# The first gate product in two halves: contraction over four feature blocks at a time, with the context's transposes between its heads

## The chip, the cores and the metric
One core of a Trainium2 chip runs the whole program in one launch. The time is the device time of an execution in microseconds; lower is better. TensorE (PE) multiplies, VectorE (DVE), ScalarE (ACT) and GpSimd (POOL) do the rest, and SyncE (SP) and GpSimd issue the DMAs. All data are float32.

## The reference
Two transformer blocks with adaptive modulation follow each other. Only the head of the first one matters here. 256 latent tokens `x` and 256 context tokens `ctx`, each 1024 wide, are normalised and modulated by a shift and a scale that come from a conditioning vector, and then multiplied by the columns of `w_in`:

```python
mod_lat = jax.nn.silu(c) @ w_ada[l] + b_ada[l]
mod_ctx = jax.nn.silu(c_ctx) @ w_ada[l] + b_ada[l]
sh1, sc1, gt1, sh2, sc2, gt2 = jnp.split(mod_lat[:, None, :], 6, axis=-1)
...
h_lat = modulate(rmsnorm(x_lat, norm_pre_mix[l]), sh1, sc1)      # h * (1 + scale) + shift
h_ctx = modulate(rmsnorm(x_ctx, norm_pre_mix[l]), csh1, csc1)
...
da_q, da_k, da_v, hg_ff, hg_fb, hg_i, hg_q, hg_g = jnp.split(h_lat @ w_in, SPLITS, axis=-1)
...
f = lb + (1.0 - lb) * jax.nn.sigmoid(z.astype(jnp.float32))      # the forget gate of hg_ff and hg_fb
```

After it come a gated recurrence and a differential attention in parallel, an output product, 16 experts with expert-choice routing, and then a second network (latent attention and a Fourier mixer) on the result.

## The kernel before
**Tiles.** Weights come in tiles of 1024 rows by 512 columns (2 MB), as eight blocks of 128 rows, into a ring of slots; the early part uses slots 0 to 3 in turn. `("ada", i)` is the i-th 512 columns of the modulation weights: ada 0 and 1 are the shift of features 0 to 511 and 512 to 1023, ada 2 and 3 the scale of the same halves. `("in", t)` is a tile of `w_in`; in 3 and in 4 are the gates of the two directions of the recurrence. SyncE walks `stream` in order (L664). For a tile that reuses a slot it first waits until the last reader of the tile before has filled its bank. Before: ada 0, 1, 2, 3, in 3, ada 6, in 4, ada 7, in 6, ada 8, in 5 and on.

**Conditioning.** `mod_product(i)` (L813) multiplies the silu of the conditioning by tile ada i on TensorE: 16 matmuls. ScalarE copies the result (`take_mod`, L1380); `mod_columns(i)` on TensorE (L824) turns it into columns, and on VectorE (L1722) adds the bias. `fold` (L1729) makes the scale ready, once for the latent set `MIX`, once for the context set `MIXC`.

**The activations.** x is normalised, turned by TensorE (`turn_input`, `turn_chunks`, L803: 16 transposes of 128x128) and copied to `hT`, feature blocks j = 0 to 7 on the partitions. When the modulation is known, VectorE modulates hT in place, eight operations of 128x256 (L1739), and signals `hT_ready`.

**The order on TensorE** (the program below in short):

```python
turn_input(0)
for i in FIRST_MODS:            # 0, 1, 2, 3
    mod_product(i)
    if i:
        mod_columns(i - 1)
...
for d in range(2):              # w_in tiles 3 and 4
    heads_out(("z", d, hp), w, (2 * hp, 2 * hp + 1), lat, T)
    if d == 0:
        turn_input(1)           # the context's transposes
    tokens_out(("zc", d, b), w, hT3, TB + b)
    mod_step(d)                 # products of ada 6, then ada 7
```

`heads_out` makes the gate of two heads in one bank, 2 x 8 matmuls of 128x256 (L794), contraction over all eight blocks of hT. `tokens_out` makes the context's gate zc, token block by token block, with 128x512 matmuls. The context's transposes are copied out of their banks, already modulated, by ScalarE (L1363, blocks 0 to 3) and VectorE (L1701, blocks 4 to 7).

**Behind it.** ScalarE takes the exponential of z and zc; VectorE makes sigmoids (a reciprocal of 128x1024 takes 6.55 us), the running sums and 1 - f; ScalarE takes logarithms (L1407, L1409). From those TensorE makes the triangle sums `dsum`, the first matmuls with `pair` as operand (L794 at 125.03). GpSimd computes the reciprocal roots of the norms and, once the last of the first ada tiles has landed, loads ctx, the rows of the lower bound, the lambda rows, subln, hgn and the mask.

**Banks.** PSUM has eight banks; `claim(name, b)` fixes at build time the order in which results take a bank, `pclaim` goes round banks 0 to 3. An engine that takes a bank waits until its last content was read.

Of the kernel before, what the change touches and what calls it, by code (L numbers as in the profile page):

```python
# [12 lines left out]
P = 128  # L13
# [97 lines left out]
FIRST_MODS = [0, 1, 2, 3]  # L111
# [22 lines left out]
def block_program(nc, a, out):  # L134
    ctx = ExitStack()
    with ctx:
# [91 lines left out]
        def mod_tile(i):  # L228
            l, o = divmod((i - 12) * TN, 3 * D)
            tile(("ada", i), wtile(a["w_ada"][0], i * TN) if i < 12 else wtile(a["w_ada_2"][l], o))  # L230

        for i in FIRST_MODS:
            mod_tile(i)

        order = iter(COLUMN_MODS)
        for t in (3, None, 4, None, 6, None, 5, None, None, 1, None, None, 0, None, None, None, None, 7, 2, None):
            if t is None:
                mod_tile(next(order))
            else:
                tile(("in", t), wtile(w_in, t * TN))  # L240
# [27 lines left out]
        def place(name, s):  # L268
            slot_of[name], turn_of[name] = s, slot_uses[s]
            slot_uses[s] += 1  # L270

        occupants = {}
        turn = 0
        for name, _ in stream:
            if name[0] == "kvctx":
# [90 lines left out]
        for i in FIRST_MODS:  # L366
            claim(("mod", i), i)
            claim(("modT", i), 4 + i)
# [6 lines left out]
        def claim_gate(d):  # L375
            for hp in range(2):
                pclaim(("z", d, hp))
            if d == 0:
# [14 lines left out]
        claim_mod(0)  # L393
# [305 lines left out]
        def _(pool):  # L699
# [26 lines left out]
            pool.wait_ge(landed[FIRST_MODS[-1]], 16)  # L726
# [64 lines left out]
        def _(pe):  # L791
# [56 lines left out]
            def turn_input(s):  # L848
                for b in range(TB):
                    pe.wait_ge(sem("normed"), 2 * s + b + 1)  # L850
                    for g in range(2):
                        turn_chunks(("xT", s, b, g), (tm3, cx3)[s][:, b, :], g)

            turn_input(0)
            pe.wait_ge(sem("silu_c"), 1)
            for i in FIRST_MODS:
                mod_product(i)
                if i:
                    mod_columns(i - 1)
            mod_columns(FIRST_MODS[-1])  # L860

            pe.wait_ge(sem("hT_ready"), 1)
# [13 lines left out]
            for d in range(2):  # L876
                w = wait_tile(pe, ("in", 3 + d))
                for hp in range(2):
                    heads_out(("z", d, hp), w, (2 * hp, 2 * hp + 1), lat, T)
                if d == 0:  # L880
                    turn_input(1)
                    for b in range(TB):
                        for g in range(2):
                            wait_copied(pe, ("xT", 1, b, g))
                for b in range(TB):
                    tokens_out(("zc", d, b), w, hT3, TB + b)
                mod_step(d)
# [451 lines left out]
        def _(act):  # L1339
# [56 lines left out]
            for d in range(2):  # L1396
                for hp in range(2):
                    o = wait_filled(act, ("z", d, hp))
                    frees(st, act.activation(kg[d][:, hp * TN:(hp + 1) * TN], o[:, :], ACT.Exp, scale=-1.0),
                          ("z", d, hp))  # L1400
# [4 lines left out]
                take_mod(COLUMN_MODS[d])  # L1405
# [253 lines left out]
        def _(dve):  # L1659
# [66 lines left out]
            def fold(s, norm, signal):  # L1726

                st.settle()
                step(dve.scalar_tensor_tensor(mc[:, s, 1, :], mc[:, s, 1, :], 1.0, norm, ALU.add, ALU.mult), signal)  # L1729
                st.settle()  # L1730

            for i in FIRST_MODS:
                mod_columns(i)
            fold(MIX, colof("pre_mix"), None)
            fold(MIXC, colof("pre_mix"), "mc_ready")
            wait_copied(dve, ("xT", 0, 1, 0))
            st.settle()
            for j in range(J):
                step(dve.tensor_scalar(hT3[:, j, 0:T], hT3[:, j, 0:T], mc[:, MIX, 1, j:j + 1], mc[:, MIX, 0, j:j + 1],  # L1739
                                       ALU.mult, ALU.add), "hT_ready" if j == J - 1 else None)  # L1740
# [47 lines left out]
            for d in range(2):  # L1788
                wait_copied(dve, ("z", d, 0))
                wait_copied(dve, ("z", d, 1))  # L1790
# [509 lines left out]
```

## Time and profile before
| | us |
|---|---|
| median of three runs | 1204.85 (1204.59 to 1205.53) |
| the profiled execution | 1199.85 |
| its span in the trace | 1198.0 |
| TensorE busy | 943.8 (79%) |
| VectorE busy | 300.7 (25%) |
| ScalarE busy | 210.6 (18%) |
| GpSimd busy | 45.5 (4%) |
| mean granted TensorE clock | 0.918 of full speed |
| moved by DMA | 310.46 MB, 259 GB/s over the span |

The profiled execution is a run of its own, 5 us shorter than the median. Its span leaves out 1.85 us at the ends. Everything between 480 and 890 us is the experts' loop, which waits for their weights; the change is in the first 80 us.

### The profile page before, as it was taken

The numbers are of one execution on the slowest core, as the hardware profiler recorded it, in microseconds if no ns is written. First come the engines' busy times: TensorE is split into PE (matmuls) and PEld (weight loads), VectorE is DVE, ScalarE is ACT, GpSimd is POOL, SyncE is SP. The second block draws the span as 40 slices with busy tenths as digits, with TensorE's granted clock in tenths as the row PEclk, the third lists the DMA queues.
The fourth block names the chain that finished last, engine by engine and source line by source line (L and its number), as shares of the span: only waits on it lengthen the run. The fifth ranks groups of instructions, "written<-read, shape, count | busy, mean of one in ns | idle before, by whom it ended". The sixth has DMA issues, their size and how long they took to land.

```text
span 1198.0 us, 11068 instructions
## 1 busy us (share of the span) xinstructions
PE 943.8 (79%) x4392; PEld 491.1 (41%) x4392; DVE 300.7 (25%) x551; ACT 210.6 (18%) x429; POOL 45.5 (4%) x98
## 2 busy tenths in 40 slices
PE   4799989999898769665666666566566988989987
PEld 2666454754544355121212212122124845534843
DVE  1299233570451333000000000000003134330002
ACT  2223221321352212000000000000003134210010
POOL 0200000000100100000000000000001000000000
PEclk9899989999899869888888888888888999999999
DMA  9943441771988309999999999999995441041000
GB/s 353 348 155 141 176 145 67 270 292 71 329 297 350 140 9 413 418 429 428 429 429 429 429 428 428 428 428 429 428 414 208 178 159 43 1 141 71 1 1 35
DMA packets 65367, 310.46 MB, mean 259 GB/s; under 512 B 2705, under 2 KB 4932, under 8 KB 52916
## 3 DMA queue, kind: packets, MB, share of 16 engines
q1 hardware_dynamic: 62836, 301.04, 62.8%
q0 software_dynamic: 2496, 8.93, 2.1%
q8 instruction: 24, 0.39, 0.1%
q14 instruction: 11, 0.09, 0.0%
HBM read 308.91 MB, written 1.05 MB: 259 GB/s over the span
## 4 chain that ended last, share of the span: by engine, by line
PE 59%; DMA 28%; DVE 6%; issue 2%; ACT 2%; SPq 1%; POOL 1%; POOLq 0%; ACTq 0%; DVEq 0%
PE bank L794 41%; DMA ring<-w_up_dram 27%; PE bank L1127 8%; PE bank L813 3%; DMA ring<-w_ada_dram 2%; PE bank L925 1%; PE bank L824 1%; PE bank L803 1%; SPq L664 1%; PE bank L1145 1%; PE bank L1259 1%; PE bank L977 1%; PE bank L1282 1%; PE bank L1158 1%; PE bank L832 1%
## 5 line engine op out<-in xcount | busy, mean ns | idle before, releaser
L1127 PE MATMUL bank<-ring,ilat 128*32 128x512 f32 x960 | 147.1, 768 | 107.4 <-DMA ring<-w_up_dram 107.3
L1127 PEld LDWEIGHTS bank<-ring,ilat 128*32 128x32 f32 x960 | 40.9, 135 | 211.8 <-issue 211.8
L794 PE MATMUL bank<-ring,kT 128*128 128x512 f32 (+1 forms) x224 | 97.7, 597 | 5.4 <-DVE kT L1701 3.4
L794 PE MATMUL bank<-ring,hT 128*128 128x512 f32 x224 | 98.8, 601 | 1.7 <-DVE hT L1701 1.7
L2131 DVE TENSOR_TENSOR state<-state,bank 64x512 f32<-64x512 f32 x16 | 11.0, 690 | 329.3 <-ACT state L1571 329.3
L794 PE MATMUL bank<-hT,ring 128*128 128x256 f32 (+1 forms) x320 | 86.5, 431 | 3.6 <-DVE hT L1739 3.6
L794 PEld LDWEIGHTS bank<-hT,ring 128*128 128x128 f32 x320 | 61.8, 195 | 28.3 <-issue 17.7
L1145 PE MATMUL bank<-ring,ilat 128*32 128x512 f32 x512 | 62.8, 633 | 11.8 <-ACT ilat L1575 11.8
L1571 ACT ACTIVATE state<-bank 64x512 f32<-64x512 f32 x16 | 9.5, 592 | 332.6 <-PE bank L1127 332.6
L794 PEld LDWEIGHTS bank<-ring,kT 128*128 128x128 f32 x224 | 43.1, 194 | 58.2 <-issue 58.2
L794 PEld LDWEIGHTS bank<-ring,hT 128*128 128x128 f32 x224 | 43.0, 193 | 55.6 <-issue 53.6
L1158 PE MATMUL bank<-state,ilat 128*128 128x512 f32 x120 | 55.1, 601 | 13.6 <-DVE state L2135 13.6
L794 PE MATMUL bank<-kT,ring 128*128 128x256 f32 x256 | 55.7, 379 | 0.0
L813 PE MATMUL bank<-ring,act 128*32 128x512 f32 x384 | 49.4, 636 | 6.7 <-DMA ring<-w_ada_dram 3.0
L794 PEld LDWEIGHTS bank<-kT,ring 128*128 128x128 f32 x256 | 48.6, 190 | 7.3 <-issue 0.8
L1158 PEld LDWEIGHTS bank<-state,ilat 128*128 128x128 f32 x120 | 21.6, 189 | 48.3 <-issue 48.3
L803 PE MATMUL bank<-const,pair 128*128 128x128 f32 x112 | 20.1, 339 | 26.6 <-DVE pair L2068 18.9
L1145 PEld LDWEIGHTS bank<-ring,ilat 128*32 128x32 f32 x512 | 15.8, 115 | 47.2 <-issue 41.9
L2135 DVE COPY state<-bank 128x512 f32<-128x512 f32 x16 | 11.1, 692 | 89.8 <-PE bank L1145 89.8
L803 PEld LDWEIGHTS bank<-const,pair 128*128 128x128 f32 x112 | 16.9, 181 | 30.7 <-DVE pair L2068 20.2
L1136 PE MATMUL bank<-const,state 128*128 128x128 f32 x64 | 11.8, 308 | 21.5 <-DVE state L2131 21.5
L794 PE MATMUL bank<-ring,gates 128*128 128x512 f32 x64 | 27.7, 593 | 1.1 <-DVE gates L2249 1.1
(315 smaller groups left out, 1007.9 us busy)
## 6 DMA issues: line engine op xcount, KB each, us to landing
ring<-w_down_dram SPq DMA_DIRECT2D x32, 2048.0 KB, 24.0
ring<-w_gate_dram SPq DMA_DIRECT2D x32, 2048.0 KB, 18.8
ring<-w_up_dram SPq DMA_DIRECT2D x32, 2048.0 KB, 23.3
ring<-w_ada_dram SPq DMA_DIRECT2D x24, 2048.0 KB, 11.4
ring<-w_in_dram SPq DMA_DIRECT2D x8, 2048.0 KB, 12.1
ring<-fno_w_in_dram SPq DMA_DIRECT2D x4, 2048.0 KB, 8.1
ring<-w_out_dram SPq DMA_DIRECT2D x2, 2048.0 KB, 8.3
ring<-mla_w_in_dram SPq DMA_DIRECT2D x2, 2048.0 KB, 21.8
```

What stands on the lines that cost most here:

```text
L664: sp.dma_start(slot_view(s, src.shape[1], src.shape[2]), src).then_inc(landed[s], 16)
L794: ins = pe.matmul(o, l, r, start=start and i == 0, stop=stop and i == len(terms) - 1)
L803: ins = pe.transpose(o[:, jj * P:(jj + 1) * P], chunk, ident)
L813: ins = pe.matmul(o[32 * q:32 * q + 32, :], act_cols[i // 12][:, j, :], w[:, j, :], start=jj == 0, stop=jj == 1)
L824: ins = pe.matmul(o[:, 2 * jj:2 * jj + 2], chunk, C("sum_columns"), start=True, stop=True)
L832: fills(pe.matmul(o[:, :], C("sum_columns")[:, 0:1].broadcast_to([P, P]), modr_of(i), start=True, stop=True), ("gt", i))
L925: ins = pe.matmul(o[:, k * P:(k + 1) * P], keys[:, c:c + P], queries[:, c:c + P], start=True, stop=True)
L977: fills(pe.matmul(o[i][:, :], q3[ps, h, b * P:(b + 1) * P], k3[ps, h, :], start=True, stop=True), ("s", b, h, i))
L1127: ins = pe.matmul(bank[0][32 * t:32 * t + 32, :], x[:, j, :], w[2 * half + t // 2][:, j % JH, n0:n0 + TN], start=j == 0, stop=j == J - 1)
L1145: ins = pe.matmul(bank[2 + n][32 * q:32 * q + 32, :], hmT[:, q, 32 * c:32 * c + 32], w[4 + c][:, q, n * TN:(n + 1) * TN], start=c == 0, st ...
L1158: ins = pe.matmul(bank[4 + 2 * b + n][:, :], m[:, b * P:(b + 1) * P], yb[n], start=first, stop=last)
L1259: fills(pe.matmul(o[:, :], ckv_all[:, b * P:(b + 1) * P], wvh[:, 4 * g:4 * g + 4, P:2 * P], start=True, stop=True), ("v2", b, g))
```

## The change
The first four ada tiles come in the order 0, 2, 1, 3, and in 3 is loaded in the third place. Shift and scale of features 0 to 511 are then known first: VectorE folds and modulates blocks 0 to 3 of hT, and TensorE contracts these four blocks for all four heads of the gate z(0), into four banks (0, 1, 5, 6) that stay open. With ada 1 and ada 3 the same is done for blocks 4 to 7, which completes the sums. After head 1 and after head 3 of this second half TensorE turns one token block of the context each. The product of ada 6 goes ahead of zc(0). in 3 stays in its slot beyond ada 6, so the slots of the later tiles are worked out by what is used up first. GpSimd's loads wait for ada 1 instead of ada 3 by name; both have the fourth place in the queue.

```diff
-FIRST_MODS = [0, 1, 2, 3]
+FIRST_MODS = [0, 2, 1, 3]
...
-        for i in FIRST_MODS:
-            mod_tile(i)
+        mod_tile(FIRST_MODS[0])
+        mod_tile(FIRST_MODS[1])
+        tile(("in", 3), wtile(w_in, 3 * TN))
+        mod_tile(FIRST_MODS[2])
+        mod_tile(FIRST_MODS[3])
...
-        for t in (3, None, 4, None, 6, None, 5, None, None, 1, None, None, 0, None, None, None, None, 7, 2, None):
+        for t in (None, 4, None, 6, None, 5, None, None, 1, None, None, 0, None, None, None, None, 7, 2, None):
...
-        turn = 0
+        tiles = [name for name, _ in stream if name[0] != "kvctx"]
+        used_up = [name for name in tiles if name != ("in", 3)]
+        used_up.insert(used_up.index(("ada", COLUMN_MODS[0])) + 1, ("in", 3))
...
-                place(name, turn % EARLY_SLOTS)
-                turn += 1
+                place(name, k if k < EARLY_SLOTS else slot_of[used_up[k - EARLY_SLOTS]])
...
-            claim(("mod", i), i)
-            claim(("modT", i), 4 + i)
+            claim(("mod", i), 2 + k % 2)
+            claim(("modT", i), (4, 7)[k % 2])
...
+                for h in range(HEADS):
+                    claim(("z", d, h), (0, 1, 5, 6)[h])
+                pb[0] = 2
...
+                claim(("mod", COLUMN_MODS[0]), 4)
...
-            pool.wait_ge(landed[FIRST_MODS[-1]], 16)
+            ada1 = ("ada", FIRST_MODS[2])
+            pool.wait_ge(landed[slot_of[ada1]], 16 * (turn_of[ada1] + 1))
...
+            def first_gate(h, half):
+
+                o = pe_take(pe, ("z", 0, h)) if half == 0 else bank[turns[("z", 0, h)][0]]
+                ins = sum_of(o[:, 0:T], [(w3[:, j, h * P:(h + 1) * P], lat[j])
+                                         for j in range(4 * half, 4 * half + 4)],
+                             start=half == 0, stop=half == 1)
+                if half:
+                    fills(ins, ("z", 0, h))
+
+            for half in range(2):
+                pair_of = FIRST_MODS[2 * half:2 * half + 2]
+                for i in pair_of:
+                    mod_product(i)
+                for i in pair_of:
+                    mod_columns(i)
+                w3 = wait_tile(pe, ("in", 3))
+                pe.wait_ge(sem("hT_ready"), half + 1)
+                for h in range(HEADS):
+                    first_gate(h, half)
+                    if half and h % 2:
+                        turn_input(1, h // 2)
+            mod_step(0)
+            for b in range(TB):
+                for g in range(2):
+                    wait_copied(pe, ("xT", 1, b, g))
+            for b in range(TB):
+                tokens_out(("zc", 0, b), w3, hT3, TB + b)
...
+                n = TN if d else T
+                for i in range(1024 // n):
+                    o = wait_filled(act, ("z", d, i))
+                    frees(st, act.activation(kg[d][:, i * n:(i + 1) * n], o[:, 0:n], ACT.Exp, scale=-1.0),
+                          ("z", d, i))
+                if d == 0:
+                    take_mod(COLUMN_MODS[0])
...
+            for half in range(2):
+                js = slice(4 * half, 4 * half + 4)
+                for i in FIRST_MODS[2 * half:2 * half + 2]:
+                    mod_columns(i)
+                fold(MIX, colof("pre_mix"), None, js)
+                if half == 0:
+                    wait_copied(dve, ("xT", 0, 1, 0))
+                for j in range(4 * half, 4 * half + 4):
+                    step(dve.tensor_scalar(hT3[:, j, 0:T], hT3[:, j, 0:T], mc[:, MIX, 1, j:j + 1],
+                                           mc[:, MIX, 0, j:j + 1], ALU.mult, ALU.add),
+                         "hT_ready" if j == 4 * half + 3 else None)
+                fold(MIXC, colof("pre_mix"), "mc_ready" if half else None, js)
```

## Rows read from the trace of the kernel before
**Rows 1.** The page: span, and the chain that ended last, by engine.
```profile
span 1198.0 us, 11068 instructions
...
PE 59%; DMA 28%; DVE 6%; issue 2%; ACT 2%; SPq 1%; POOL 1%; POOLq 0%; ACTq 0%; DVEq 0%
```
**Rows 2.** TensorE's waits from 0 to 140 us: total, times, longest.
```profile
PE bank L794 <- DVE hT L1739: 3.6, 1, 3.6
PE bank L813 <- DMA ring<-w_ada_dram: 3.0, 2, 2.2
```
**Rows 3.** The chain in order of time, 10 to 76 us: start, us, what.
```profile
10.16 20.07 DMA ring<-w_ada_dram
...
37.69 16.21 PE bank L794 x64
...
58.83 15.67 PE bank L794 x32
```
**Rows 4.** The timeline, 18 to 91 us: start, us, what [idle before <- releaser].
```profile
17.98 3.69 PE L813 MATMUL bank<-ring,act 128*32 128x512 f32 x32
...
24.86 3.60 PE L813 MATMUL bank<-ring,act 128*32 128x512 f32 x16 [2.21 <-DMA ring<-w_ada_dram]
...
30.28 1.92 PE L813 MATMUL bank<-ring,act 128*32 128x512 f32 x16 [0.83 <-DMA ring<-w_ada_dram]
...
33.05 1.03 PE L824 MATMUL bank<-const,modr 128*128 128x2 f32 x8
...
34.96 2.67 DVE L1739 TENSOR_SCALAR hT<-hT,modc 128x256 f32<-128x256 f32 x8
...
37.69 4.55 PE L794 MATMUL bank<-hT,ring 128*128 128x256 f32 x10 [3.61 <-DVE hT L1739]
...
43.57 1.42 DVE L1693 TENSOR_SCALAR pair<-pair,small 128x1024 f32<-128x1024 f32 x2 [5.94 <-POOL small L720]
...
53.73 1.04 PE L803 MATMUL bank<-const,pair 128*128 128x128 f32 x8
...
76.28 14.08 PE L794 MATMUL bank<-hT,ring 128*128 128x256 f32 x64
...
90.20 13.90 PE L794 MATMUL bank<-ring,hT 128*128 128x512 f32 x32
```
**Rows 5.** SyncE's issues of in 3, ada 6, in 4: start, and time to landing.
```profile
L664 SPq DMA_DIRECT2D ring<-w_in_dram x1: 373/373/373, 20.0 to 20.0; - x1
DMA to landing us min/median/max: 16.6/16.6/16.6
...
L664 SPq DMA_DIRECT2D ring<-w_ada_dram x1: 5036/5036/5036, 21.7 to 21.7; - x1
DMA to landing us min/median/max: 31.8/31.8/31.8
...
L664 SPq DMA_DIRECT2D ring<-w_in_dram x1: 4283/4283/4283, 28.5 to 28.5; - x1
DMA to landing us min/median/max: 30.5/30.5/30.5
```
**Rows 6.** Two stretches: busy time by engine, granted clock, DMA share, GB/s.
```profile
41.00:42.00 1.00, 1.00 (x4) 0.82 (x3) 0.00 (x0) 0.97 (x3) 0.00 (x0) 0.50 1.04 403
42.00:43.00 1.00, 1.00 (x6) 0.85 (x6) 0.00 (x0) 0.32 (x2) 0.42 (x2) 0.99 1.01 379
```
**Rows 7.** VectorE's chain: hgn's landing, its ends in the timeline, its wait.
```profile
L735 POOL DMA_DIRECT2D hgn<-hg_norm_dram x1: 537/537/537, 35.0 to 35.0; - x1
DMA to landing us min/median/max: 15.5/15.5/15.5
...
57.21 1.36 DVE L1701 TENSOR_SCALAR hT<-bank,modc 128x128 f32<-128x128 f32 x4 [1.03 <-PE bank L803]
...
115.77 1.06 ACT L1409 ACTIVATE pair<-pair 128x1024 f32<-128x1024 f32 x1 [5.08 <-DVE pair L1805]
...
125.03 0.30 PEld L794 LDWEIGHTS bank<-pair,const 128*128 128x128 f32 x2 [0.84 <-issue]
...
DVE ring L1820 <- ACT ring L1417: 6.5, 2, 5.2
```

More of the change, by code:

```diff
@@ L365, in block_program @@
                 claim(("xT", 0, b, g), 2 + g)
[L366 to L368 removed]
+        for k, i in enumerate(FIRST_MODS):
+            claim(("mod", i), 2 + k % 2)
+            claim(("modT", i), (4, 7)[k % 2])
         pb = [0]
@@ L375, in claim_gate @@
         def claim_gate(d):
-            for hp in range(2):
-                pclaim(("z", d, hp))
-            if d == 0:
+            if d:
+                for hp in range(2):
+                    pclaim(("z", d, hp))
+            else:
+                for h in range(HEADS):
+                    claim(("z", d, h), (0, 1, 5, 6)[h])
+                pb[0] = 2
                 for b in range(TB):
@@ L847, in _, with turn_input @@
             fills(pe.transpose(o[:, 0:N_BIAS], bias_rows, ident[0:N_BIAS, 0:N_BIAS]), "bias_rows")
[L848 to L854, printed above, removed]
-            pe.wait_ge(sem("silu_c"), 1)
[L856 to L862, printed above, removed]
+            def turn_input(s, b):
+                pe.wait_ge(sem("normed"), 2 * s + b + 1)
+                for g in range(2):
+                    turn_chunks(("xT", s, b, g), (tm3, cx3)[s][:, b, :], g)
+            for b in range(TB):
+                turn_input(0, b)
+            pe.wait_ge(sem("silu_c"), 1)
             def heads_out(name, w, hs, rhs, n):
@@ L875, in _ @@
             lat = [hT3[:, j, 0:T] for j in range(J)]
[L876 to L887, printed above, removed]
+            def first_gate(h, half):
[19 more added lines that the diff above has]
+            for b in range(TB):
+                for g in range(2):
+                    wait_copied(pe, ("xT", 1, b, g))
+            for b in range(TB):
+                tokens_out(("zc", 0, b), w3, hT3, TB + b)
+            w = wait_tile(pe, ("in", 4))
+            for hp in range(2):
+                heads_out(("z", 1, hp), w, (2 * hp, 2 * hp + 1), lat, T)
+            for b in range(TB):
+                tokens_out(("zc", 1, b), w, hT3, TB + b)
+            mod_step(1)
             w = wait_tile(pe, ("in", 6))
@@ L1724, in mod_columns, with fold @@
                     frees(st, ins, ("modT", i)) if r == len(sets) - 1 else step(ins)
-            def fold(s, norm, signal):
+            def fold(s, norm, signal, js=slice(0, J)):
                 st.settle()
-                step(dve.scalar_tensor_tensor(mc[:, s, 1, :], mc[:, s, 1, :], 1.0, norm, ALU.add, ALU.mult), signal)
+                step(dve.scalar_tensor_tensor(mc[:, s, 1, js], mc[:, s, 1, js], 1.0, norm[:, js], ALU.add, ALU.mult),
+                     signal)
                 st.settle()
[L1732 to L1740, printed above, removed]
+            for half in range(2):
[10 more added lines that the diff above has]
+                fold(MIXC, colof("pre_mix"), "mc_ready" if half else None, js)
             input_norm(1)
@@ L1788, in _ @@
             for d in range(2):
-                wait_copied(dve, ("z", d, 0))
-                wait_copied(dve, ("z", d, 1))
+                for i in range(2 if d else HEADS):
+                    wait_copied(dve, ("z", d, i))
                 sigmoid_in_place(kg[d])
```

11 lines of the change are left out of this document (4 added, 7 removed).

## The prediction
> **What bounds the kernel now.** I read the page first for the shape of the span: the chain of work that ended last is TensorE for 59% and DMA for 28%, and no other engine has more than 6% of it [rows 1]. All that the change touches lies in the first 80 us, so the next view is TensorE's waits up to 140 us. After the start-up (x normalised and turned, until 18 us) the large ones are 3.0 us for ada tiles and 3.6 us for the modulated hT [rows 2]. The chain in order of time says the same of who sets the pace: the ada tiles arriving until 30.2, then 16.2 us of the first gate product (z,0) from 37.7 on, then from 58.8 its context part (zc,0), 15.7 us [rows 3]. So DMA sets the pace up to about 30 us and TensorE after it. A microsecond saved before 76 us reaches the end if nothing behind it has less slack. The views after that are the timeline (what one of each costs, and what released it), the landing times of the transfers, and the clock by stretches.
>
> **The path now, in terms.** Ada 3, last of the four, lands at 10.16 + 20.07 = 30.2 [rows 3] and its product starts at 30.28; columns end at 33.05 + 1.03 = 34.1; the eight modulations start at 34.96 and take 2.67; the 64 gate matmuls run from 37.69 to 53.9. Then turning and copying the context costs until 58.83 with TensorE half idle (two batches of about 1.05), zc takes 15.67, the product of ada 6 1.85, and the second gate starts at 76.28 [rows 3, 4]. I use that instant, "second gate starts", as the meter.
>
> **The clock in these terms.** Ten of the gate matmuls took 4.55 us, 455 ns each, while 64 of the same shape at 76.28 took 14.08, 220 ns each [rows 4]. The granted clock is 0.50 (the 1.2 GHz level) at 41 to 42 and 0.99 (2.4 GHz) a microsecond later [rows 6]: TensorE had idled 3.6 us before 37.69, and the slow start costs 16.21 - 14.08 = 2.1 us. zc lost 15.67 - 13.90 = 1.8 the same way, and the product of ada 2, after 2.2 us idle, took 3.60 instead of 1.92 [rows 3, 4].
>
> **The change, part by part.** The queue now brings ada 0, ada 2, in 3, ada 1, ada 3, ada 6. The places in the queue stay as they are, only the names change, so I read the landings by place: third place 24.9 and fourth 30.2 (the products that waited for ada 2 and ada 3 [rows 4]), fifth, now ada 3, 20.02 + 16.6 = 36.6, sixth, still ada 6, 21.73 + 31.8 = 53.5 [rows 5]. The GpSimd queue waits for ada 1, which has the fourth place, so its context load starts at 30.5 as before and meets ada 3 where it met in 3. The last tile that the conditioning needs thus comes 6.4 us later; that is the price. What it buys:
>
> First half. Products of ada 0 and ada 2 run back to back from 17.98 (3.69 for 32, as now [rows 4]), columns follow at 21.6; two times 1.05 makes 23.7. VectorE now needs 34.96 - 34.08 = 0.88 from the columns' end to the first modulation, two folds included; one fold now comes after, so I take 0.6 (estimate), and four modulations are half of 2.67, 1.3. hT's first half is ready at 25.6, after in 3 (24.9). The 32 matmuls cost 32 x 0.22 = 7.0 at full clock and 32 x 0.455 = 14.6 if all run at the low level. TensorE will have idled 2 us, so I take the slow start that is seen today, +2.1: done at 25.7 + 9.2 = 34.9. This hides under the wait for ada 3 up to 34.7, since the product of ada 1 (1.85) must still be done before 36.6.
>
> Second half. Product of ada 1 to 36.7, of ada 3 to 38.6, both columns 1.9 (now 32.2 to 34.1) to 40.5, VectorE 0.6 + 1.3 to 42.4. Matmuls 7.0 + 2.1 = 9.2 to 51.6 (bounds 7.0 and 14.6). Between the heads stand two batches of turned context, 2 x 1.05 = 2.1, to 53.7. Each batch needs a normalised half of the context, which VectorE had at 43.57 + 1.42 = 45.0 [rows 4]; the first batch stands at about 48, so no wait, unless GpSimd's root comes later than the 43.5 of now. The first batch's copies are covered by the heads 2 and 3 (3.5 us), the second's by the product of ada 6, moved ahead of zc for that: last copy 53.7 + 0.05 + 1.36 = 55.1, the last two as at 57.2 now [rows 7], product done at 53.7 + 1.85 = 55.6 (ada 6 has landed at 53.5, 0.2 before). With that cover gone the copies would cost 1.4. zc runs without a slow start, 13.9, to 69.5. Second gate: 69.5 against 76.28, **6.8 us earlier**. The same sum by terms: 46.1 us from the last tile to the second gate become 32.9, and 6.4 is given back.
>
> Edits costed at nothing. Four exponentials of 256 instead of two of 512 on ScalarE, and its copy of the ada 6 product before zc's: a quarter to one microsecond more work, on an engine that takes them after VectorE's constants, some 10 us after the gate banks are filled. Four folds instead of two: some 0.4 us on VectorE behind the signal that TensorE waits for. Bank numbers: two more banks for z, all later claims move on by one; each bank is still retaken four claims later. SyncE: in 4 now waits for the product of ada 1 (36.7 instead of 28.5) with ada 7 and in 6 queued behind it, but the ring still moves ada 6 until 53.5; in 4 landed at 28.5 + 30.5 = 59.0 [rows 5] and is needed at 69.5. in 6 is asked for at 55.6 instead of 74.5 and is needed only behind the second gate and its context part, at 69.5 + 14.1 + 13.9 = 97.5. The order in which the first expert's tiles take the four slots changes too; I expect nothing of it, as expert 0 waits for none of them now (its wait would show in the chain as a DMA of w_gate).
>
> Does it survive? VectorE's long chain of reciprocals starts when the context is modulated, at 57.21 + 1.36 = 58.6 now and at 55.1 by my sum, so it comes only 3.5 earlier. It ends in the ScalarE logarithm at 115.77 + 1.06 = 116.8, which the triangle products need at 125.03 [rows 7]. New: 113.3 against 118.2, so 4.9 of the 8.2 us of slack are left. VectorE then idled 5.2 us for ScalarE's exponentials of those products [rows 7]: it waits for TensorE, not the other way round. The side loads of VectorE's chain end with hgn at 35.03 + 15.5 = 50.5 [rows 7], before 55.1. From there tiles are asked for by TensorE's own progress, and everything moves as a block.
>
> **A rule against a row.** In 3 needed 6.4 us in the fifth place, against 5.4 between the tiles ahead of it (24.86 to 30.28), with the context load beside it [rows 4, 5]; the tile after it needed 16.9. The Trainium skill (DMA: Bandwidth & Descriptors, Queues, rings and completion order) says that each DMA engine goes round-robin between queues, a packet at a time. The row of in 3 agrees only weakly, that of ada 6 strongly. By that rule at equal shares the fifth tile would take twice 5.4 and land at 41.1, and the gain would shrink to some 2.3; the row of in 3 gives 6.8, and I go by it, since both queues hold the same bytes in the same place.
>
> **The rivals.**
> The clock. Either half could run wholly at 1.2 GHz: +5.4, gain 1.4 (1203.4); or zc also starts slowly: +1.8, gain 5.0 (1199.8). For it: three slow starts in today's 60 us. Against it: each ended within some 4.5 us of work, and TensorE now idles less before zc. The Trainium skill (TensorE: Matmul & The Clock Gate, What's actually happening) makes the reduced clock the default that activity lifts; the rows bear it out, and they have the price.
> Absorbed later. If VectorE's chain had no slack, only its 3.5 would remain: 1201.4. Against it stand the 8.2 us.
> Slower. Ada 3 shares the fate of ada 6 of today, 16.9 us in transfer, if the GpSimd loads beside it take their share earlier: it lands at 47.1, +10.5, time 1208.5. It decides from a landing of 43.4 on. Today's fifth place says 36.6.
> More. Without slow starts TensorE is ready at 51.6 instead of 53.7, and ada 6 may land sooner because in 4 stands in the ring later: gain up to 8.9, 1196.0. With ada 6 at 53.5 that path stops at 7.0.
>
> **How the numbers follow.** The profiled execution took 1199.85 (span 1198.0), the median run 1204.85; I take the difference as it is, so 1204.85 - 6.8 = 1198.0 (profiled: span 1191.2). Chances: forecast 0.68 (gain 5.8 to 7.6), clock 0.13, absorbed 0.06, slower 0.04, more 0.09. The range goes from the "more" case, 1196.0, over zc's slow start to the absorbed case, 1201.5; it leaves out a half wholly at the low clock and the late tile. This kernel's measurement can tell about 0.2%, 2.4 us, from no change. Faster by over that: forecast, more, absorbed and most of clock, 0.90; within 0.05; slower 0.05.
>
> **What would show it.** First gate matmul near 25.7; product of ada 3 starting at 36.6 to 36.8, released by DMA or by nothing; second half from 42.4; no wait for the context's copies; the product of ada 6 ending near 55.6; second gate near 69.5, and the experts' first product earlier by the same. Wrong would be: a landing of ada 3 or ada 6 some microseconds later, clock 0.50 through a half, or a wait for VectorE at the triangle products.

## The result, and the profile after

The changed kernel takes 1195.49 us in the median of four runs (1194.97 to 1196.32), the kernel before 1205.19 in four (1204.59 to 1205.65): 9.7 us less, ratio 0.992, interval 0.9903 to 0.9938. The forecast was 1198.0 with a range from 1196.0. Timed twice more, beside fresh runs of the kernel before, the gain was 7.6 us (1196.91 against 1204.47, ratio 0.9946, interval 0.9929 to 0.9963) and 8.9 us (1195.89 against 1204.78, ratio 0.9935, interval 0.9915 to 0.9955). So the first measurement lies at the high end, but all three are above the 6.8 of the sum. 1195.49 is 0.5 us under the lower end of the range.

The profiled execution took 1195.64 (span 1193.8). TensorE's waits from 0 to 140 us in the changed kernel, to be read against [rows 2]:

```profile
PE bank L804 <- DVE hT L1771: 2.0, 1, 2.0
PE bank L804 <- issue: 2.0, 1, 2.0
```

L804 is the line that was L794, L823 was L813, L834 was L824, and L813 is now the line of the transposes (L803 before). The 3.6 us wait ahead of one whole gate has become two of 2.0, one ahead of each half. The waits for ada tiles are gone from the list, and so is the wait for the modulated context, which in the kernel before was

```profile
PE bank L794 <- DVE hT L1701: 1.7, 1, 1.7
```

The stretch from 18 us on in order of time (start, us, what, idle before and its releaser), to be read against [rows 4]:

```profile
18.23 4.79 PE L823 MATMUL bank<-ring,act 128*32 128x512 f32 x32
...
23.87 1.03 PE L834 MATMUL bank<-const,modr 128*128 128x2 f32 x8
...
26.89 8.83 PE L804 MATMUL bank<-hT,ring 128*128 128x256 f32 x32 [1.98 <-issue]
...
35.65 3.64 PE L823 MATMUL bank<-ring,act 128*32 128x512 f32 x32
...
40.13 1.03 PE L834 MATMUL bank<-const,modr 128*128 128x2 f32 x8
...
43.20 5.38 PE L804 MATMUL bank<-hT,ring 128*128 128x256 f32 x16 [2.03 <-DVE hT L1771]
...
48.41 1.04 PE L813 MATMUL bank<-const,pair 128*128 128x128 f32 x8
...
49.28 3.62 PE L804 MATMUL bank<-hT,ring 128*128 128x256 f32 x16
...
52.74 1.04 PE L813 MATMUL bank<-const,pair 128*128 128x128 f32 x8
...
53.70 0.16 PEld L823 LDWEIGHTS bank<-ring,act 128*32 128x32 f32 x8 [0.17 <-DMA ring<-w_ada_dram]
...
55.56 14.00 PE L804 MATMUL bank<-ring,hT 128*128 128x512 f32 x32
```

The second half starts at 43.2 (42.4 forecast), the product of ada 6 at 53.7 (53.7), released by the DMA of its tile; zc runs 55.6 to 69.4 without a slow start, and the second gate starts at 69.4 (69.5). In the chain of the same stretch TensorE has no gap left between its pieces from 43.2 on:

```profile
43.20 5.38 PE bank L804 x16
48.57 0.87 PE bank L813 x8
49.45 3.46 PE bank L804 x16
52.90 0.87 PE bank L813 x8
53.77 1.85 PE bank L823 x16
```

By "head" I mean everything up to the start of the second gate. The new head came out as the sum had it, and yet the gain is larger. Stranger still, the two profiles' spans differ by 4.2 us only (1198.0 and 1193.8), less than the sum. That the new profile took what its kernel usually takes (1195.64 against 1195.49), while the profile of before took 5 us less than the runs around it (1199.85 against 1204.85), is where the experiments began.

### The profile page after: what moved, and what is told of

It reads as the page before. It is cut to its first block, busy times and chain, and to the rows that moved or that the text cites. A ratio compares the mean times of both kernels' runs of the same rounds, so it can differ in the third digit from the quotient of the medians.

```text
span 1193.8 us, 11077 instructions
## 1 busy us (share of the span) xinstructions
PE 942.1 (79%) x4392; PEld 491.6 (41%) x4392; DVE 300.9 (25%) x553; ACT 210.4 (18%) x431; POOL 45.5 (4%) x98
## 4 chain that ended last, share of the span: by engine, by line
PE 60%; DMA 28%; DVE 5%; issue 2%; ACT 2%; SPq 1%; POOL 1%; POOLq 0%; ACTq 0%; DVEq 0%
PE bank L804 41%; DMA ring<-w_up_dram 27%; PE bank L1153 8%; PE bank L823 3%; DMA ring<-w_in_dram 2%; PE bank L813 1%; PE bank L951 1%; PE bank L834 1%; PE bank L1171 1%; PE bank L1285 1%; PE bank L1308 1%; PE bank L1184 1%; PE bank L842 1%; ACT junk L1371 1%; PE bank L1003 1%
## 5 line engine op out<-in xcount | busy, mean ns | idle before, releaser
L804 PE MATMUL bank<-ring,kT 128*128 128x512 f32 (+1 forms) x224 | 97.5, 596 | 5.3 <-DVE kT L1731 3.4
L804 PE MATMUL bank<-ring,hT 128*128 128x512 f32 x224 | 97.2, 593 | 0.0
L804 PE MATMUL bank<-hT,ring 128*128 128x256 f32 (+1 forms) x320 | 88.0, 436 | 4.0 <-DVE hT L1771 2.0
L804 PEld LDWEIGHTS bank<-hT,ring 128*128 128x128 f32 x320 | 62.6, 198 | 28.7 <-issue 21.5
L804 PEld LDWEIGHTS bank<-ring,kT 128*128 128x128 f32 x224 | 43.1, 194 | 58.2 <-issue 58.2
L804 PEld LDWEIGHTS bank<-ring,hT 128*128 128x128 f32 x224 | 42.4, 190 | 53.4 <-issue 52.5
L804 PE MATMUL bank<-kT,ring 128*128 128x256 f32 x256 | 55.7, 379 | 0.0
L823 PE MATMUL bank<-ring,act 128*32 128x512 f32 x384 | 48.6, 630 | 4.6 <-DVE pair L1986 3.2
L804 PEld LDWEIGHTS bank<-kT,ring 128*128 128x128 f32 x256 | 48.6, 190 | 7.3 <-issue 0.8
L813 PE MATMUL bank<-const,pair 128*128 128x128 f32 x112 | 21.5, 356 | 25.2 <-DVE pair L2102 18.9
L813 PEld LDWEIGHTS bank<-const,pair 128*128 128x128 f32 x112 | 18.2, 191 | 29.2 <-DVE pair L2102 20.2
L804 PE MATMUL bank<-ring,gates 128*128 128x512 f32 x64 | 27.7, 594 | 1.1 <-DVE gates L2283 1.1
```

The source lines that it names most:

```text
L804: ins = pe.matmul(o, l, r, start=start and i == 0, stop=stop and i == len(terms) - 1)
L813: ins = pe.transpose(o[:, jj * P:(jj + 1) * P], chunk, ident)
L823: ins = pe.matmul(o[32 * q:32 * q + 32, :], act_cols[i // 12][:, j, :], w[:, j, :], start=jj == 0, stop=jj == 1)
```

## The experiments

**The kernel before and the changed one, again.** Neither is edited.

> The kernel before, unchanged, profiled and timed again. What is open: the changed kernel's second gate starts at 69.5, 6.8 us earlier, as forecast, but its span is only 4.3 us shorter (1193.8 against 1198.0) while its median is 9.7 us below that of the kernel before (1195.5 against 1205.2). The profiled execution of the kernel before took 1199.85, 5 us under all its other runs; that of the changed kernel took 1195.64, like its other runs. Theory A: the profiled execution of before was uncommon; a new profile takes about 1204 to 1206 and shows the 5 us inside the span, at one place (the clock in a stretch, or the time per expert in the loop, 29.4 us each). Rival B: the 5 us lie outside the span; then the spans of all runs are near 1198 and the times near 1205. Rival C: it differs from chip to chip; then all runs on this chip are alike.

Measured: 1204.58 in the median of 12 executions, from 1200.59 to 1208.74, the time and the span of each differing by the same 1.8 us, so the spread is in the span. Rival B falls, and C too, since the spread shows within one chip. The mean granted clock was 0.919 for the shortest and 0.911 for the longest. Its new profile took 1201.54, again a short one; of 94 executions of the kernel before in this study the median is 1204.65, and only one of them (1199.70) is shorter than the first profile's 1199.85. The new profile differs from [rows 4] ahead of the gate:

```profile
30.64 3.24 PE L813 MATMUL bank<-ring,act 128*32 128x512 f32 x16 [1.21 <-DMA ring<-w_ada_dram]
...
39.36 16.15 PE L794 MATMUL bank<-hT,ring 128*128 128x256 f32 x64 [3.60 <-DVE hT L1739]
...
77.90 14.08 PE L794 MATMUL bank<-hT,ring 128*128 128x256 f32 x64
```

The product of ada 3 started 0.4 us later and took 3.24 us instead of 1.92, and everything from there to the second gate (77.9) is 1.6 to 1.7 us later.

> The changed kernel, unchanged, profiled and timed again on the same chip. If the first measurement holds: 1195 to 1196, ratio 0.992. Theory A (my term of 6.8 is right for the head of the kernel and some 3 us come from a later place that depends on when things start): the second gate starts near 69.5 again, and the later place shows where this profile and the new one of before part. Rival (noise between executions): the ratio comes out nearer to 0.9944, which 6.8 us would give.

Measured: 1196.91 (1194.95 to 1199.45, six executions). Second gate at 69.3. In this profile the product of ada 3 waited for its tile until 37.24, 0.6 after the 36.6 that I had taken.

**One part alone.** The halves without the context's part (ScalarE's copy of the ada 6 product moves back with it):

```diff
                     first_gate(h, half)
-                    if half and h % 2:
-                        turn_input(1, h // 2)
-            mod_step(0)
+            for b in range(TB):
+                turn_input(1, b)
...
                 tokens_out(("zc", 0, b), w3, hT3, TB + b)
+            mod_step(0)
...
```

> The changed kernel without its second part: the context is turned after the last head, and the product of ada 6 stands behind zc again; the two halves of the contraction stay. By the terms: second half ends near 51.5 to 52, turning and copying 4.9 us, zc with a slow start 15.7, product 1.85: second gate at 74.5, 1.7 us before that of the kernel before. Theory of additive terms: median 1203.5, the change of the loads and halves alone is worth 1 to 2 us. Rival (the gain beyond 6.8 comes with the halves or with the new order of slots): 1200 to 1201.

Measured: 1199.16 (1197.36 to 1200.89), ratio 0.9962 (0.9948 to 0.9976), 5.3 us where I had 1.7. In its profile the second gate starts at 73.6, 0.9 before the terms, mostly because zc had no slow start.

The context's part without the halves, from the kernel before (the bank of the ada 6 product and ScalarE's copy of it move as in the change):

```diff
                     heads_out(("z", d, hp), w, (2 * hp, 2 * hp + 1), lat, T)
+                    if d == 0:
+                        turn_input(1, hp)
                 if d == 0:
-                    turn_input(1)
+                    mod_step(0)
...
                     tokens_out(("zc", d, b), w, hT3, TB + b)
-                mod_step(d)
+                if d:
+                    mod_step(1)
```

> The kernel before with the second part alone: one token block of the context is turned after each pair of heads of the first gate, and the product of ada 6 goes ahead of zc, with its bank and ScalarE's copy moved as in the change; loads, conditioning and contraction as before. By the terms: gate and transposes 37.7 + 16.2 + 2.1 = 56.0, product 57.9, zc without a slow start 71.8: second gate 4.5 us earlier, median 1200.7. Rival (the gain beyond 6.8 comes with this part): 1197 to 1198.

Measured: 1203.34 (1198.12 to 1207.1), ratio 0.9995 (0.9974 to 1.0016), so by the whole kernel not told from no change. Its profile, the shortest of the 12 executions (1198.12), has the second gate at 73.0, 1.2 after the terms: the product of ada 3 took 3.42 and the gate started at 39.4.

**Keeping TensorE busy, too long.** Extra matmuls of constants, whose results nobody reads, in the waits:

```diff
+            def fill(n):
+                for _ in range(n):
+                    pe.matmul(bank[3][:, :], const[:, 0:P], const[:, 0:TN], start=True, stop=True)
...
+                if i == 1:
+                    wait_copied(pe, ("xT", 0, 1, 1))
+                    fill(4)
+                if i == 2:
+                    fill(1)
             mod_columns(FIRST_MODS[-1])
+            fill(7)
```

> The kernel before, with extra matmuls of constants (128x512, into a bank that is free, their result is never read) in TensorE's three waits ahead of the first gate: four behind the columns of ada 0, one behind those of ada 1, seven behind those of ada 3; 0.43 us each at full clock, so they fit into waits of 2.2, 0.9 and 3.6 us. Nothing else changes. What is open: the kernel before runs anywhere from 1199.7 to 1211.0, the changed one and the one with halves only within 3 to 5 us, and low granted clocks (0.909 to 0.914) go with the long executions. Theory A (TensorE's low clock ahead of and in the first gate makes both the mean and the spread of the kernel before): gate in 14.1 instead of 16.2, executions within some 4 us, median at most 1201. Rival B (the long executions lose their time elsewhere, behind the head): spread and median stay, 1203 to 1204.5.

Measured: 1202.49 (1198.34 to 1206.29), ratio 0.9976 (0.9956 to 0.9995). Neither theory's number, and the reason is mine: a float32 matmul of this program is two instructions in the trace, so seven calls are 14 records and 6.25 us, not 3.0, and the gate started 2.7 us late.

```profile
34.25 6.25 PE L859 MATMUL bank<-const 128*128 128x512 f32 x14
...
40.34 13.98 PE L794 MATMUL bank<-hT,ring 128*128 128x256 f32 x64
```

The gate itself ran in 13.98, but in the same profile zc took 16.95 instead of 15.67 (granted clock 0.50 until 65.6 us), so what the gate won was lost in part behind it. The same fill, `fill(4)` behind each pair of columns, in the changed kernel:

> The changed kernel with four such extra matmuls behind each pair of columns, in the two waits of 2.0 us ahead of the two halves. By the terms the second half loses its slow start (1.6 to 2.1 us), so TensorE has turned the context near 51.6 instead of 53.6; but the product of ada 6 then waits for its tile, which lands near 53.5. Theory of the floor (that landing holds the path): second gate 69.3 again, median 0 to 0.5 us under the changed kernel's 1196.5. Rival (no floor, the tile comes sooner since in 4 is asked for later): second gate near 67.5, median 1194.5 to 1195.

Measured: 1194.96 (1191.34 to 1196.87), with the second half held back to 44.1; the second gate started at 68.5.

**The halves' cover taken away.**

```diff
-                w3 = wait_tile(pe, ("in", 3))
-                pe.wait_ge(sem("hT_ready"), half + 1)
-                for h in range(HEADS):
-                    first_gate(h, half)
-                    if half and h % 2:
-                        turn_input(1, h // 2)
+            w3 = wait_tile(pe, ("in", 3))
+            pe.wait_ge(sem("hT_ready"), 2)
+            for h in range(HEADS):
+                for half in range(2):
+                    first_gate(h, half)
+                if h % 2:
+                    turn_input(1, h // 2)
```

> The changed kernel with the first gate in one piece: both pairs of columns and both modulated halves of hT are waited for, then each head contracts all eight blocks; the order of the loads, of the context's transposes and of the product of ada 6 stay as in the change. It prices the 6.4 us by which the last ada tile comes later, with the halves' cover taken away. By the terms: 43.2 + 16.2 + 2.1 = 61.5, product 63.3, zc to 77.2: second gate 7.8 us behind the change's. Theory (terms of the head add up): median 1204 to 1205, that is no gain over the kernel before. Rival (the change's lower mean and spread come from the new order of loads, not from the halves): 1200 or less, executions within 4 us.

Measured: 1205.52 (1202.75 to 1207.14), ratio 1.0013 (1.0 to 1.0026). The new order of loads and the context's part together, without the halves, bring nothing over the kernel before: the later tile costs at least what the context's part gives. In the profile the second gate starts at 79.6, 2.4 after the terms. The low clock lies on the path here too, over the last product, both column turns and the first part of the gate:

```profile
36.76 3.11 PE L823 MATMUL bank<-ring,act 128*32 128x512 f32 x16 [2.61 <-DMA ring<-w_ada_dram]
39.80 1.87 PE L834 MATMUL bank<-const,vda 128*128 128x2 f32 x8
41.52 1.85 PE L834 MATMUL bank<-const,modr 128*128 128x2 f32 x8
45.35 9.94 PE L804 MATMUL bank<-hT,ring 128*128 128x256 f32 x32 [1.98 <-issue]
```

> The kernel before, one more profile. Its executions range from 1199.7 to 1211; the two profiles so far took 1199.85 and 1201.54. If this one takes over 1203, it shows where a long execution loses its time: theory A, ahead of the second gate (76.3 and 77.9 so far, 80 or more then) with the clock at 0.50 through much of the first gate; rival B, behind it.

Measured: 1203.81. Second gate at 76.6, so this one lost its time behind the head: 3.7 of the 4.0 us that it is longer than the first profile. One of the places, 16 transposes, in the first profile of before and in this one:

```profile
375.74 1.94 PE L803 MATMUL bank<-const,pair 128*128 128x128 f32 x16 [1.60 <-DVE qT L1998]
```

```profile
376.97 3.57 PE L803 MATMUL bank<-const,pair 128*128 128x128 f32 x16 [1.60 <-DVE qT L1998]
377.00:380.00 3.00, 3.00 (x15) 3.00 (x16) 0.47 (x1) 1.40 (x3) 0.00 (x0) 0.50 0.98 421
```

The last line is a stretch, with the granted clock third from its end: 0.50, where the first profile has 1.00 (376 to 378). Both waited 1.60 us for the same operation just before.

From the second gate to the end the profiles of before took 1121.7, 1121.8 and 1125.4 us; those of the changed kernel 1124.4, 1126.5 and 1123.9 (the third is of the last run below). All 13 profiles of full kernels in this study lie between 1121.2 and 1126.5, in no order by kernel. That part has the same code in all and varies by up to 5 us. Another place is the first expert's first product, in the first profile of before and in that of the changed kernel, each with its clock:

```profile
443.51 7.07 PE L1127 MATMUL bank<-ring,gates 128*32 128x512 f32 x64 [1.65 <-issue]
444.00:446.00 2.00, 2.00 (x24) 0.73 (x20) 0.00 (x0) 0.72 (x1) 0.00 (x0) 1.00 0.00 0
```

```profile
437.36 8.58 PE L1153 MATMUL bank<-ring,gates 128*32 128x512 f32 x64 [1.64 <-issue]
438.00:440.00 2.00, 2.00 (x16) 0.56 (x12) 0.00 (x0) 0.56 (x1) 0.00 (x0) 0.50 0.00 0
```

The two spans differ by only 4.2 while the second gates differ by 6.9, because the first profile of before was 2.7 us shorter behind the head; 1.5 of these lie here.

**The heads cut off.** All engines stop where the second gate would start; the edit ends each engine's program there and stores x, once the last result of TensorE is there (the product of ada 6, or the second token block of zc where that comes last). Left out are also the constants that VectorE and ScalarE prepare beside the head. The edit of the kernel before, in part:

```diff
-            for name, src in stream:
+            for name, src in stream[:8]:
...
+            wait_filled(sp, ("mod", COLUMN_MODS[0]))
+            for b in range(TB):
+                sp.dma_start(out[0].rearrange("(b p) d -> p b d", p=P)[:, b, :], xr3[:, b, :])\
+                  .then_inc(sem("stored"), 16)
+            sp.wait_ge(sem("stored"), 16 * TB)
+            return
```

> Only the head of the kernel before: every engine stops where the second gate would start, and x is stored as the output; left out are the constants of VectorE and ScalarE for the gates, and everything behind. It measures, in every execution and not in a profile alone, how long the head takes and how much it varies. In the three profiles of before the second gate started at 76.3, 77.9 and 76.6, so with some 5 us for the store the span is about 81 to 83. What is open: the full kernel's executions reach from 1199.7 to 1211.0, those of the changed kernel from 1195.0 to 1199.5, though the profiles differ by 6.8 to 7.6 in the head. Theory A (the head of before has long executions, its slow starts fall differently from one to the next): executions between 80 and 88, a third of them over 84. Rival B (the spread arises behind the head): all within 2 us.

> Only the head of the changed kernel, cut at the same place and with the same parts left out. The profiles have 69.4 and 69.3 for the second gate, so the span is about 74 to 75. Theory A: all executions within 2 us, so that head before less head after is 6.8 in the shortest executions and 8 to 10 in the mean. Rival B: the difference is 7 in every execution, and what is beyond it in the medians of the full kernels comes from behind the head.

> Only the head of the kernel with the halves alone, cut in the same way. Its profile has 73.6 for the second gate: span about 78 to 79. Theory A: narrow like the changed kernel's, since the wait of 3.6 us ahead of a whole gate is gone, which would account for its median (1199.2) being 5.3 under the kernel before, where the profiles differ by 2.7 to 4.3. Rival B: as wide as all the others.

> Only the head of the kernel with the context's part alone, cut in the same way. Its profile has 73.0 for the second gate: span about 78. Theory A: wide, 77 to 85, like the head of before, since it keeps the wait of 3.6 us ahead of a whole gate; that would account for its median (1203.3) being only 1.1 under the kernel before, where the terms give 4.5. Rival B: as narrow as the others, and the 3.4 us are lost behind the head.

Measured, each over five or six executions (the same 6.1 us lie in each between the second gate's instant and the execution's time: 78.7 and 84.79 in the profile of the head of before, 68.9 and 74.98 in that of the changed head):

| head of | median | lowest to highest | less than before, medians | less than before, lowest |
|---|---|---|---|---|
| the kernel before | 84.17 | 82.71 to 85.41 | | |
| halves alone | 80.00 | 78.51 to 80.30 | 4.2 | 4.2 |
| context's part alone | 80.17 | 77.87 to 81.77 | 4.0 | 4.8 |
| the changed kernel | 75.36 | 74.98 to 75.61 | 8.8 | 7.7 |

The head's own gain is 8.8 us by the medians, between the three measurements of the full kernels, and 7.7 by the shortest executions; both are above the 6.8 of the sum. By the scatter of five or six executions the 8.8 is good to about 1 us, the 4.2 and the 4.0 to some 1 to 1.5. By the median of these cut heads the second gate of before starts at 84.17 - 6.1 = 78.1, not at 76.3. The three full profiles of before have it at 76.3, 77.9 and 76.6, so 78.1 stands on the cut heads alone. The spread of the head of before is 2.7 us and not the 8 that I had expected of theory A; the changed head's is 0.6. The profile of the head of before took 84.79:

```profile
30.58 3.64 PE L821 MATMUL bank<-ring,act 128*32 128x512 f32 x16 [0.72 <-DMA ring<-w_ada_dram]
34.15 1.87 PE L832 MATMUL bank<-const,vda 128*128 128x2 f32 x8
35.88 1.85 PE L832 MATMUL bank<-const,modr 128*128 128x2 f32 x8
41.33 16.59 PE L802 MATMUL bank<-hT,ring 128*128 128x256 f32 x64 [3.60 <-DVE hT L1741]
```

and its granted clock (third from the end of each line) over three of those microseconds:

```profile
32.00:33.00 1.00, 1.00 (x8) 0.20 (x4) 0.00 (x0) 0.00 (x0) 1.00 (x3) 0.50 1.06 391
35.00:36.00 1.00, 1.00 (x6) 1.00 (x6) 0.00 (x0) 0.00 (x0) 1.00 (x3) 0.50 1.04 397
41.00:42.00 1.00, 0.67 (x2) 0.58 (x3) 0.28 (x1) 0.97 (x3) 0.00 (x0) 0.50 1.02 397
```

The last product and both column turns lie at 0.50, the 1.2 GHz level, and they lie on the path: product 3.64 instead of 1.92, columns 3.6 instead of 1.9, the gate starting at 41.3 instead of 37.7, and slow at first all the same. In return zc had no slow start in this profile:

```profile
62.85 13.97 PE L802 MATMUL bank<-ring,hT 128*128 128x512 f32 x32 [1.66 <-DVE hT L1703]
```

It waited the same 1.66 us for the same operation as in the full profiles, where it took 15.67. So where the low clock falls differs from one execution to the next, and with it what it costs.

**Fitting extra matmuls.** As above with `fill(2)`, `fill(1)`, `fill(4)`; in the changed kernel `fill(2)` behind each pair of columns. First the cut head of before with them, then the full kernels.

> The head of the kernel before, cut as above, with extra matmuls of constants in TensorE's waits that this time fit them: two (four records, 1.8 us) behind the columns of ada 0, one behind those of ada 1, four (3.5 us) behind those of ada 3. Theory A (the low clock in the product and columns of ada 3 and in the gate makes the head of before long and uneven): the product of ada 3 takes 1.9, gate in 14.0 from 37.9, zc with a slow start, second gate near 74.5; executions within 1.5 us around 80 to 81, against 82.7 to 85.4 without them. Rival (the landing of ada 3 or the context makes the long ones): 83 to 85 as before.

Measured: 80.62 (79.04 to 80.76), 3.5 us under the head of before (which was timed on another chip; the full kernel's medians on the two, 1204.27 and 1204.78, differ by 0.5). In the profile, a 79.04 one, the product of ada 3 and the gate run at full clock:

```profile
30.65 1.92 PE L821 MATMUL bank<-ring,act 128*32 128x512 f32 x16 [1.57 <-DMA ring<-w_ada_dram]
...
38.08 14.06 PE L802 MATMUL bank<-hT,ring 128*128 128x256 f32 x64
```

```profile
32.00:33.00 1.00, 1.00 (x13) 0.50 (x5) 0.00 (x0) 0.30 (x1) 1.00 (x3) 1.00 1.05 385
```

zc too ran without a slow start (13.97). Two executions took 79.0 to 79.1 and four 80.6 to 80.8, some 1.6 us apart, about what a slow zc costs; that the four had it is my estimate, as only one was profiled.

> The whole kernel before with the same fitting extra matmuls. Theory A: the head's 3.5 us come through, median 1200.5 to 1201.5. If the spread of 1199.7 to 1211 arises in the head it shrinks to 4 us; if behind it, it stays at 8 to 10.

Measured: 1198.39 (1196.08 to 1207.68, 12 executions), ratio 0.996 (0.9939 to 0.998). The median falls by 6.4 us, more than the head's 3.5; nine of the 12 lie within 4.3 us, but three at 1203.8 to 1207.7 remain. In its profile (1197.54) the second gate starts at 74.5, and from there to the end it took 1121.2 us, the shortest of all; what the median gained beyond the head lies behind it and is not explained.

> The changed kernel with two extra matmuls (1.8 us) in each of its two waits of 2.0 us. The overlong ones of before held the second half back by 1.0 us and still gave 1195.0; fitting ones let it start at 43.1 and end 1.0 earlier. Theory (the landing of ada 6 no longer holds anything, it came before 52.8 in that run): second gate near 67.6, median 1194 to 1194.5. Rival (floor at 53.5): second gate 69.3, median as e6.

Measured: 1194.90 (1191.54 to 1197.13), ratio 0.992 (0.9893 to 0.9946). In its profile the second half is at full clock and TensorE has turned the context at 51.8, and then it waits (start, us, what, idle before and its releaser):

```profile
50.75 1.04 PE L813 MATMUL bank<-const,pair 128*128 128x128 f32 x8
53.39 1.92 PE L823 MATMUL bank<-ring,act 128*32 128x512 f32 x16 [1.60 <-DMA ring<-w_ada_dram]
...
69.08 13.98 PE L804 MATMUL bank<-hT,ring 128*128 128x256 f32 x64
```

The floor is there: second gate at 69.1, the slow start of the second half is paid into a wait for ada 6. (The overlong fill's 68.5 was possible because the tile had landed by 52.8 in that profile.)

> The changed kernel unchanged, on the chip of the two runs above. 1195.5 to 1197; tells whether the 9.7 us of the first measurement or the 7.6 of the second is the usual difference: by the heads cut off it is 8.8.

Measured: 1195.89 (1194.93 to 1201.22, nine executions). Second gate at 69.7. The version with extra matmuls is 1.0 below it on the same chip; with intervals some 5 to 6 us wide on both against the kernel before, that is not told from nothing.

## Why the prediction was wrong

**The change's own side held.** Landings by place in the queue: in 3 there before it is needed, ada 3 in time for its product (37.2 in the second profile, 36.8 with the whole gate, 36.6 forecast; the 41.1 of equal shares did not come), ada 6 at 53.6 where 53.5 was forecast. First half from 26.9 (25.7 forecast; the products of ada 0 and ada 2 ran partly at the low clock, 4.79 instead of 3.69), done at 35.7 and so nearly hidden, second half from 43.2 (42.4), 10.5 us with its transposes instead of 11.3 because part of the slow start was gone, product of ada 6 at 53.7, zc without a slow start, second gate 69.4 (69.5). VectorE's chain did not become the bound: its logarithm ended 5.1 us ahead of the triangle products (4.9 forecast):

```profile
111.91 1.06 ACT L1439 ACTIVATE pair<-pair 128x1024 f32<-128x1024 f32 x1 [8.22 <-DVE pair L1839]
...
118.04 0.30 PEld L804 LDWEIGHTS bank<-pair,const 128*128 128x128 f32 x2 [0.84 <-issue]
```

SyncE's later issue of in 4 and the other order of slots showed in no wait. The price of 6.4 us for the later last tile shows with the whole gate under the new order of loads: the product of ada 3 starts at 36.8 there instead of 30.3, and the time, 1205.5, is no gain over the kernel before.

**The step that failed** is the term for the old head, and the sentence that ties it to the median: "The profiled execution took 1199.85 (span 1198.0), the median run 1204.85; I take the difference as it is". The sum starts from the second gate at 76.28 and has 2.1 us for the slow start of the first gate as the only cost of the low clock up to the end of that gate. Both come from one profile, which was among the shortest executions of its kernel, and the 5 us to the median were no constant that adds to both kernels alike. By the medians of the cut heads the old head reaches the second gate at 78.1, 1.8 us later, and the new one at 69.3. That makes 8.8 us where my sum had 76.3 - 69.5 = 6.8. In the full profiles the same is seen in part: on average 76.9 against 69.4, 7.5 us.

With 8.8 in place of 6.8 the sum would give 1204.85 - 8.8 = 1196.05, at the very end of the range. What is left to 1195.49 is within the scatter of the changed kernel's three medians (1195.49, 1195.89, 1196.91).

**What is in the 1.8.** In [rows 4] the product of ada 3 (1.92) and its columns run at full clock and only the gate starts slowly. In the second full profile the low clock covers most of the product of ada 3, in the head's profile its columns too, all of it on the path, because nothing else is left to wait for. In the third full profile it covers neither. Extra matmuls that only keep TensorE busy in the waits shorten the cut head by 3.5 us, of which my sum had 2.1 as the gate's slow start; the rest, 1.4, is what the profile did not show. That the low clock is the cause is thus shown for some 3.5 us of the cut head; how these divide over product, columns and gate in the median is not measured. The changed kernel hides these places: its first products and half of the gate run under the wait for ada 3, and its head varies by 0.6 us.

**The rivals.** "More" gave the right time (1196.0) for a wrong reason: it took slow starts away from the new kernel. With fitting extra matmuls these did go, and the second gate stayed at 69.1, because ada 6 landed no sooner (53.4 there); the missing time was to be counted in the old kernel. That its price came out close is luck. "Absorbed" and "slower" did not come about. The clock rival had the right mechanism on the wrong side as well: I priced it for the changed kernel alone, though the three slow starts that spoke for it were those of before.

**The parts.** In the heads, halves alone give 4.2 and the context's part 4.0, together 8.2 of the 8.8, which is the same within their scatter. My terms had 1.7 and 4.5. So the term of the halves is the one that was too small. Two things in the profiles speak for why: the halves take the first products, and half of the gate, out from behind the low clock, and zc then had no slow start (1.7 us), in the full profile and in the cut one. Which of the two counts for how much no run here separates; the head of before had a zc without a slow start once too.

**What stays open.** The full kernel before varies by 11 us in 94 executions, its head by 2.7 in six; the rest arises behind the second gate. Three places there, each at the low clock in one profile and at full clock in another, are the 16 transposes above (1.6 us), the first expert's product above (1.5), and a row of matmuls in the third profile of before from 254.1 to 257.6 us (granted clock 0.51, 1.00 in the first profile; 1.6). What decides in an execution where the low clock falls was not found. The kernel before kept long executions with its head filled, and the kernel with the context's part alone gained 4.0 in the head but 1.1 in the full median. A whole gate behind a long wait does not explain it: with the whole gate under the new order of loads the 12 executions lie within 4.4 us. So I can't say how much of the differences between 7.6, 8.9 and 9.7 is chance. That the head's gain is above 6.8 is shown; what lies beyond 8.8 is not.

## What to carry to other kernels

Before a sum from one profile is set against a median, compare the profiled execution's own time with the other runs: if it is shorter or longer by as much as the gain in question, part of what is missing may lie in the stretch that is changed. Cutting the kernel off behind the stretch and timing that in several executions measures it without the noise of the rest. In this kernel, work on the path behind TensorE's waits often cost more than its full-clock duration (the product of ada 3 took 1.92, 3.24 and 3.64 us in three profiles); splitting the product so that half of it filled the wait took that work off the path.

## What the runs showed of the hardware that was not expected

One and the same program took from 1199.7 to 1211.0 us in 94 executions, and the longer ones had, on the whole, the lower mean granted clock (0.918 at 1199.7, 0.909 at 1211.0). Behind the same wait of 1.60 us the same 16 transposes took 1.94 us in one execution and 3.57 in another. In the profile of the head of before the granted clock stayed at 0.50 from 26 to 46 us, with TensorE busy for 79% of that time. Extra matmuls whose results nobody reads took 3.5 us off a head of 84, and 6.4 us off the full kernel's median.
